# The alpha/beta columns of a projection in four 32-column groups of the array, in fp32

## The chip, the cores and the metric

One core of one Trainium2 chip runs the whole kernel. The metric is device time in microseconds (us), taken as the median of several runs; the profile is one execution taken apart by the hardware profiler.

## The reference, cut to what matters

One layer of a streaming encoder over 1024 positions of width 1024. A conditioning vector gives shift, scale and gate (`mod = silu(c) @ W_ada + b_ada`), the normed input is modulated, and one wide projection feeds both branches:

```python
mod = (cond @ w_ada[l] + b_ada[l])[:, None, :]
sh1, sc1, gt1, sh2, sc2, gt2 = jnp.split(mod, N_MOD, axis=-1)
h = rmsnorm(x, norm1_g[l]) * (1.0 + sc1) + sh1
proj = h @ w_in[l]
qa, ka, va, qkvb, zb, bb, ab, ga, gb = jnp.split(proj, IN_SPLITS, axis=-1)
...
beta = jax.nn.sigmoid(b_raw.astype(jnp.float32))
g = -jnp.exp(a_log.astype(jnp.float32)) * jax.nn.softplus(
    a_raw.astype(jnp.float32) + dt_bias.astype(jnp.float32))
```

`bb` and `ab` (beta and alpha, 4 heads each) are 8 columns of the projection. `qkvb` goes through a causal convolution over four taps and SiLU. Chunked attention, a gated delta rule, the branch merge, an output projection and a SwiGLU feed-forward follow; the change does not touch them.

## The kernel before, in words

**Layout.** Activations lie transposed, features on the 128 partitions, as `act_hi` and `act_lo` of [128, 8, 1024]: the value rounded to fp32r, and what rounding left. The projection goes by units of 128 output columns. A unit's weights (512 KB) land in one of four slots of `w_raw`; ScalarE rounds them to `w_hi` (`split_hi`, line 1666), VectorE forms `w_lo` (`split_lo`, line 2115), both with two slots, and TensorE does three fp32r products (hi by hi, hi by lo, lo by hi) for each of 8 blocks k and each half of 512 positions: 48 matmuls a unit (`dense_k`, line 1164), into `ps[unit % 2]`.

**The start.** Unit 0 holds the 8 alpha/beta columns and 120 others that nobody reads; unit 1 is the first convolved unit. Modulation comes in four parts n; part n gives shift and scale of blocks k = 2n and 2n+1. For a part VectorE sums five of the eight row blocks of `w_ada` (`ada_sum`, lines 2134 and 2136), and TensorE adds the other three and that sum in fp32, four products for each of four column blocks (`modulation`, lines 1217 and 1219). VectorE then scales x (line 2160), ScalarE makes `act_hi` (line 1690), VectorE `act_lo` (line 2165). `units01(n)` multiplies units 0 and 1 with blocks 2n and 2n+1 as they come ready; `beat` fills time on TensorE with small products that nobody reads.

**Units from 2 on** need their split weights (`wlo_ready`) and the bank of the unit two before (`est_ready`). Evacuation of a convolved unit d is a chain: ScalarE copies the bank to `est[d % 2]` (line 1741), then splits the weights of unit d+2; VectorE forms their low part and only then adds three taps (line 2216); ScalarE takes tanh (line 1745); VectorE finishes (line 2221) and raises `est_ready`; GpSimd stores the result (line 1017). From unit 3 on the copy waits for the store of unit d-2:

```python
                    else:
                        act.wait_ge(est_stored[ds % 2], 16 * ((ds - 1) // 2))
```

Ahead of unit 6 TensorE also waits for gate products of GpSimd (line 1263), which follow the store of unit 4.

**DMA order.** Loads are issued by SyncE (SP) in the order of its program, each after its own wait; a waiting instruction holds up all behind it. After the parts of `w_ada` come the weights of units 2 to 5, then a store of x transposed (`xT_d`, 4096 KB, line 615), a store of the attention's bias table (`ext_d`, 1536 KB, line 617, read from 8 partitions, each 128 times over), and the weights of unit 6 (which wait for `wlo_ready` 3) and of the units behind.

```python
                if d == 5:

                    sp.wait_ge(xt_read, NT)
                    sp.dma_start(xT_d.rearrange("(k p) t -> p k t", p=P), xT0[:, :, :]).then_inc(xT_stored, 16)
                    sp.wait_ge(ext_ready, 1)
                    sp.dma_start(ext_d.rearrange("h (p n) -> h p n", n=EXT),
                                 ext[:, :].unsqueeze(1).broadcast_to([A_H, P, EXT])).then_inc(ext_stored, 16)
```

Of the kernel before, what the change touches and what calls it, by code (L numbers as in the profile page):

```python
# [110 lines left out]
def hybrid_layer(nc, x, c, w_ada, b_ada, norm1_g, norm2_g, w_in, rel_rev, w_conv, a_log, dt_bias,  # L111
                 gdn_norm_g, w_branch_a, w_branch_b, w_out, w_ffn_in, w_ffn_out, final_g, out):
    with ExitStack() as ctx:
# [42 lines left out]
        incl = sb("incl", [P, P])  # L156
        after = sb("after", [P, P])
        lvl = sb("lvl", [P, 2, P])
        vT = sb("vT", [P, V_ROWS])
# [375 lines left out]

        ACT_X = (3, 6)

        def ada_count(n):
# [6 lines left out]
        def _(sp):  # L545
# [29 lines left out]
            for t in range(NT):  # L575
                load_x(t)
            load_ada(1)
            for d in range(2):
                load_unit(d, 0, w_in_v, C_AB if d == 0 else C_QKVB + group(1) * P)
            sp.dma_start(rrow[:, :], rel_rev).then_inc(rel_in, 16)  # L580
# [28 lines left out]

            for d in range(2, D_A):  # L610
                load_unit(d, 0, w_in_v, C_QKVB + group(d) * P)
                if d == 5:
# [358 lines left out]
        def _(pool):  # L971
            for s in (yb_free, ya_free):
# [15 lines left out]
                               base=-1, pattern=[[-1, P]], channel_multiplier=1).then_inc(consts_ready, 1)  # L988

            for n, b in enumerate((BLK, 2 * BLK)):  # L990
                odd = lvl[:, n, :].rearrange("p (n two b) -> p n two b", two=2, b=b)[:, :, 1, :]
                nb = P // (2 * b)
                ch.link(pool.memset(odd, 1.0))

                ch.link(pool.affine_select(out=odd, in_=odd, compare_op=ALU.is_ge, fill=0.0, base=0,
                                           pattern=[[-2 * b, nb], [0, b]], channel_multiplier=1))
                ch.link(pool.affine_select(out=odd, in_=odd, compare_op=ALU.is_ge, fill=0.0, base=b - 1,
                                           pattern=[[2 * b, nb], [0, b]], channel_multiplier=-1))
# [157 lines left out]
        def _(pe):  # L1156
# [23 lines left out]
            def in_step(k0, k1):  # L1180
# [3 lines left out]
                return steps + [(d, k) for d in range(2) for k in range(max(k0, 6), k1)]  # L1184

            def units01(n):
                for d, k in in_step(2 * n, 2 * n + 2):
                    if d == 0:
                        pe.wait_ge(lo_ready, k + 1)
                    ins = dense_k(d, k, ps[d], act_hi[:, k, :], act_lo[:, k, :], k == 0, k == 7)  # L1190
                    if k == 7:
                        ins.then_inc(dense_mm, 1)

# [14 lines left out]
            def modulation(n):  # L1208

                pe.wait_ge(ada_in[n], ada_count(n))  # L1210
                pe.wait_ge(asum_ready, n + 1)
                if n:
                    pe.wait_ge(mod_ready, n)
                for q in range(4):
                    dst = gps[:, q * P:(q + 1) * P]
                    for k in range(5, KT):
                        pe.matmul(dst, ada_row(n, k)[:, q * P:(q + 1) * P], cs[:, k:k + 1].broadcast_to([P, P]),
                                  start=(k == 5), stop=False)
                    ins = pe.matmul(dst, asum[:, n % 2, q * P:(q + 1) * P], ones[:, :], start=False, stop=True)
                ins.then_inc(mod_mm, 1)  # L1220
# [14 lines left out]
            modulation(1)  # L1235
            beat(8)
            pe.wait_ge(xt_read, NT)
# [7 lines left out]
            for d in range(2, D_CONV):  # L1245
                for k in range(KT):
                    unit_k(d, 0, k, ps[d % 2])
                if d == 2:

                    pe.wait_ge(ab_read, 1)  # L1250
                    pe.wait_ge(mod_ready, 1)
                    for t in range(NT):
                        ins = pe.transpose(gps[:, t * 8:(t + 1) * 8], est[0:8, 0, t * P:(t + 1) * P],
                                           ident[0:8, 0:8])
                    ins.then_inc(abT_mm, 1)
# [402 lines left out]
        def _(act):  # L1658
# [15 lines left out]
            for t in range(NT):  # L1674
# [5 lines left out]
                if t in ACT_X:  # L1680
                    act.wait_ge(xt_mm, t + 1)
                    act.wait_ge(xt_read, t)
                    act.activation(xT0[:, :, t * P:(t + 1) * P], ps[t % 2][:, :].rearrange("p (k q) -> p k q", k=KT),
                                   ACT.Copy).then_inc(xt_read, 1)
            act.wait_ge(misc_in, 32)
            act.activation(negA[:, :], negA[:, :], ACT.Exp).then_inc(act_chain, 1)
            for n in range(4):
                for k in (2 * n, 2 * n + 1):
                    act.wait_ge(xn_ready, k + 1)
                    act.activation(act_hi[:, k, :], est[:, k % 2, :], ACT.Identity,  # L1690
                                   bias=modT[:, SH1 + k:SH1 + k + 1]).then_inc(hi_ready, 1)
                    if n == 0:
                        split_hi(k)

# [52 lines left out]
            for d in range(D_CONV):  # L1747
                if d == 0:
                    split_hi(2)
                    act.wait_ge(lo_ready, KT)  # L1750
                    act.activation(est[0:8, 0, :], ps[0][0:8, :], ACT.Copy).then_inc(ab_read, 1)
                    continue
# [355 lines left out]
        def _(dve):  # L2108
# [21 lines left out]
            def ada_sum(n):  # L2130
# [3 lines left out]
                ch.link(dve.tensor_scalar(dst, ada_row(n, 0), cs[:, 0:1], None, ALU.mult))  # L2134
                for k in range(1, 5):
                    ins = dve.scalar_tensor_tensor(dst, ada_row(n, k), cs[:, k:k + 1], dst, ALU.mult, ALU.add)
                    if k < 4:
                        ch.link(ins)
# [14 lines left out]
            dve.wait_ge(xt_read, NT)  # L2153
            ada_sum(1)

# [16 lines left out]
            for n in range(4):  # L2172
# [11 lines left out]
                for k in (2 * n, 2 * n + 1):  # L2184
                    norm_scale(k, xT0[:, k, :], gs[:, k:k + 1], aS[:, :], 0)
                if n == 0:
                    split_lo(0)
                    split_lo(1)
                for k in (2 * n, 2 * n + 1):
# [605 lines left out]
```

## Time and profile before

| | |
|---|---|
| median of 3 runs | 1663.96 us (1660.57 to 1665.55) |
| profiled execution, its own time | 1665.2 us |
| its span | 1662.4 us |
| TensorE (PE) busy | 1613.8 us, 97% |
| weight loads (PEld) busy | 1330.6 us, 80% |
| VectorE (DVE) busy | 923.6 us, 56% |
| ScalarE (ACT) busy | 638.8 us, 38% |
| GpSimd (POOL) busy | 268.2 us, 16% |
| chain that ended last, PE's share | 79% |

Times in the trace are microseconds from the start of the span. Matmuls are pipelined, so a group's busy time counts the overlap of neighbours once, and the distance from one start to the next is what a matmul costs. An fp32 product shows as two matmul instructions, an fp32r product as one.

### The profile page before, as it was taken

How to read it: one execution, taken by the hardware profiler on the slowest of the kernel's cores; microseconds unless marked ns; L12 is line 12 of the kernel's file. 1: busy time of each engine (PE TensorE's matmuls, PEld its weight loads, DVE VectorE, ACT ScalarE, POOL GpSimd, SP SyncE). 2: the span in 40 equal slices, each digit the busy share in tenths (PEclk: the TensorE clock that was granted, in tenths of full speed). 3: DMA queues.
4: the chain of work that ended last, by engine and by line, in shares of the span. 5: the costliest groups of instructions: out<-in, count | busy, mean ns of one | idle time of the engine just before them, and what ended most of it. 6: DMA issues, size and time to landing. Idle time of an engine off the chain costs nothing.

```text
span 1662.4 us, 24103 instructions
## 1 busy us (share of the span) xinstructions
PE 1613.8 (97%) x8235; PEld 1330.6 (80%) x8235; DVE 923.6 (56%) x1455; ACT 638.8 (38%) x1308; POOL 268.2 (16%) x284
## 2 busy tenths in 40 slices
PE   5999999999999999999999998999999999999997
PEld 5877878888878787877788887888888888888886
DVE  5777655345444444444653388866666666434424
ACT  4234455555544344444211234333333333322413
POOL 1026571011110101000000012422233220000000
PEclk9999999999999999999999999999999999999999
DMA  9745666555723333422646321222222223653412
GB/s 301 214 114 189 210 188 208 172 181 155 244 87 123 96 107 103 126 95 76 216 134 214 101 64 60 93 88 89 88 76 76 77 87 127 228 174 124 151 45 102
DMA packets 223875, 224.46 MB, mean 135 GB/s; under 512 B 18057, under 2 KB 189194, under 8 KB 223818
## 3 DMA queue, kind: packets, MB, share of 16 engines
q1 hardware_dynamic: 216762, 198.29, 38.1%
q0 software_dynamic: 7056, 25.43, 4.0%
q8 instruction: 33, 0.54, 0.1%
q14 instruction: 24, 0.20, 0.0%
HBM read 163.13 MB, written 60.56 MB: 135 GB/s over the span
## 4 chain that ended last, share of the span: by engine, by line
PE 79%; DVE 3%; DMA 3%; ACT 1%; issue 1%; SPq 0%; DVEq 0%; POOLq 0%; ACTq 0%
PE pm L1560 23%; PE pm L1574 14%; PE pd L1424 11%; PE ps L1164 9%; PE pm L1164 8%; PE sc L1377 2%; PE tT L1400 2%; DMA w_raw<-in_w_in_dram 2%; PE tT L1389 2%; PE pm L1514 1%; PE pm L1472 1%; PE gps L1314 1%; DMA yst<-yb_d 1%; PE gps L1330 1%; PE gps L1348 1%
## 5 line engine op out<-in xcount | busy, mean ns | idle before, releaser
L1164 PE MATMUL ps<-act_hi,w_hi 128*128 128x512 f32 x464 | 155.4, 416 | 3.8 <-DVE act_lo L2165 2.6
L2115 DVE TENSOR_TENSOR w_lo<-w_raw,w_hi 128x1024 fp32r<-128x1024 f32 x61 | 75.7, 1241 | 129.0 <-ACT w_hi L1666 119.2
L1164 PE MATMUL ps<-act_lo,w_hi 128*128 128x512 f32 x464 | 144.9, 394 | 0.0
L1164 PE MATMUL ps<-act_hi,w_lo 128*128 128x512 f32 x464 | 144.5, 393 | 0.0
L1574 PE MATMUL pm<-act_hi,w_hi 128*128 128x512 f32 x352 | 137.2, 390 | 0.0
L1574 PE MATMUL pm<-act_hi,w_lo 128*128 128x512 f32 x352 | 137.0, 389 | 0.0
L1574 PE MATMUL pm<-act_lo,w_hi 128*128 128x512 f32 x352 | 136.9, 389 | 0.0
L1560 PE MATMUL pm<-act_hi,w_hi 128*128 128x512 f32 x320 | 125.7, 393 | 4.7 <-DVE act_lo L2555 3.8
L1560 PE MATMUL pm<-act_lo,w_hi 128*128 128x512 f32 x320 | 125.5, 392 | 0.0
L1560 PE MATMUL pm<-act_hi,w_lo 128*128 128x512 f32 x320 | 125.4, 392 | 0.0
L1424 PE MATMUL pd<-act_hi,w_hi 128*128 128x512 f32 x256 | 111.3, 435 | 0.0
L1164 PEld LDWEIGHTS ps<-act_hi,w_lo 128*128 128x128 f32 x464 | 88.0, 190 | 19.3
L1164 PEld LDWEIGHTS ps<-act_lo,w_hi 128*128 128x128 f32 x464 | 87.7, 189 | 19.4
L1424 PE MATMUL pd<-act_hi,w_lo 128*128 128x512 f32 x256 | 101.0, 394 | 0.0
L1424 PE MATMUL pd<-act_lo,w_hi 128*128 128x512 f32 x256 | 100.3, 392 | 0.0
L1164 PEld LDWEIGHTS ps<-act_hi,w_hi 128*128 128x128 f32 x464 | 81.6, 191 | 20.0 <-issue 7.3
L2673 DVE TENSOR_TENSOR w_lo<-w_raw,w_hi 128x512 fp32r<-128x512 f32 x44 | 30.4, 692 | 117.2 <-ACT w_hi L2017 117.1
L1140 POOL TENSOR_TENSOR est<-w_raw 128x512 f32<-128x512 f32 x20 | 26.3, 1316 | 421.7 <-DVE w_lo L2547 230.2
L1560 PE MATMUL pm<-t_hi,w_hi 128*128 128x512 f32 x240 | 93.4, 389 | 0.0
L1560 PE MATMUL pm<-t_lo,w_hi 128*128 128x512 f32 x240 | 93.4, 389 | 0.0
L1560 PE MATMUL pm<-t_hi,w_lo 128*128 128x512 f32 x240 | 93.4, 389 | 0.0
L1666 ACT ACTIVATE w_hi<-w_raw 128x1024 fp32r<-128x1024 f32 x61 | 64.4, 1055 | 62.7 <-PE pm L1164 49.6
(363 smaller groups left out, 3450.7 us busy)
## 6 DMA issues: line engine op xcount, KB each, us to landing
w_raw<-in_w_in_dram SPq DMA_DIRECT2D x45, 512.0 KB, 5.9
w_raw<-in_w_ffn_in_dram SPq DMA_DIRECT2D x44, 512.0 KB, 3.8
h_raw<-h_d SPq DMA_DIRECT2D x36, 512.0 KB, 3.5
a_raw<-in_w_ada_dram SPq DMA_DIRECT2D x32, 512.0 KB, 4.5
w_raw<-in_w_ffn_out_dram SPq DMA_DIRECT2D x44, 256.0 KB, 3.9
h_d<-hid SPq DMA_DIRECT2D x21, 512.0 KB, 2.7
pk_d<-pk SPq DMA_DIRECT2D x8, 768.0 KB, 3.6
qkva_d<-est POOLq DMA_DIRECT2D x12, 512.0 KB, 6.7
```

The costliest lines, as they stand in the source:

```text
L1140: pool.tensor_tensor(s1, upw[:, 0:4], upw[:, 4:8], ALU.add).then_inc(mix_ready, 1)
L1164: ins = pe.matmul(dst[:, cols], wt[:, ds % 2, k, :], at[:, cols], start=(first and n == 0), stop=(last and n == 2))
L1314: ins = pe.matmul(hd(gps, h), gst[:, (0 if q == Q_QS else 4) + h, :], hd(St, h), start=True, stop=True)
L1377: ins = pe.matmul(score_cols(e, c0, c1), ast[rows, 0, j * P:(j + 1) * P], ast[rows, 1, k0 + c0:k0 + c1], start=True, stop=True)
L1389: ins = pe.transpose(tT[:, kt * P:(kt + 1) * P], Pm[:, e, kt * P:(kt + 1) * P], ident[:, :])
L1400: ins = pe.matmul(tT[rows, 0:P], V[:, j - nk_ + 1 + kt, rows], PT[:, e, kt * P:(kt + 1) * P], start=(kt == 0), stop=(kt == nk_ - 1))
L1424: ins = pe.matmul(pd[:, half(h)], wt[:, ds % 2, kk, :], at[:, kk, half(h)], start=(kk == 0 and n == 0), stop=(kk == KT - 1 and n == 2))
L1560: ins = pe.matmul(bank(n, o), wt[:, c, :], at, start=(c == 0 and x == 0), stop=(c == 3 and x == 2))
L1574: ins = pe.matmul(out_bank(b, h), wt[:, b, :], at[:, j % 8, half(h)], start=(t % NF == 0 and x == 0), stop=(t % NF == NF - 1 and x == 2))
L1666: act.activation(w_hi[:, ds % 2], w_raw[:, ds % NR], ACT.Copy).then_inc(whi_ready, 1)
L2115: dve.tensor_tensor(w_lo[:, ds % 2], w_raw[:, ds % NR], w_hi[:, ds % 2].bitcast(F32), ALU.subtract)\
L2673: dve.tensor_tensor(lo, w_raw[:, raw_o(t) % NR, 0:4], hi.bitcast(F32), ALU.subtract)\
```

## The change

- **Unit 0.** Only 32 columns of its weights are loaded (8 of them are used). They are not split: TensorE multiplies `w_raw` in fp32 with `act_hi` and with `act_lo`. The 16 pairs (block k, hi or lo) are dealt over four groups of 32 output partitions of the same bank, so the array holds four narrow products; the two halves of a pair stand one after the other. `ab_part(n)` has eight such products and comes between unit 1's blocks 2n and 2n+1. The bank's four groups are added when they are transposed: eight fp32 products with `sel` (four identities stacked, made by GpSimd) in place of eight transposes of an 8-row tile.
- **Loads.** The weights of units 0 and 1 are issued ahead of part 1 of `w_ada`. The load of unit 4, which takes unit 0's slot of `w_raw`, waits for unit 0's last product (`dense_mm` 1) in place of its split.
- **Splits.** Unit 1's weights are split as soon as x is read; two counters are raised in place of unit 0's.
- **Modulation.** VectorE sums (5, 0, 4, 4) row blocks in place of (5, 5, 5, 5); TensorE takes the rest. Eight `beat` products go.

```diff
@@ -155,6 +155,7 @@
         after = sb("after", [P, P])
+        sel = sb("sel", [P, 2 * B_H])
         lvl = sb("lvl", [P, 2, P])
@@ -534,6 +535,8 @@
         ACT_X = (3, 6)
+        AB_COLS = 32
+        SUM_ROWS = (5, 0, 4, 4)
@@ -574,9 +577,9 @@
                 load_x(t)
+            sp.dma_start(w_raw[:, 0, :, 0:AB_COLS], w_in_v[:, :, C_AB:C_AB + AB_COLS]).then_inc(raw_in[0], 16)
+            load_unit(1, 0, w_in_v, C_QKVB + group(1) * P)
             load_ada(1)
-            for d in range(2):
-                load_unit(d, 0, w_in_v, C_AB if d == 0 else C_QKVB + group(1) * P)
             sp.dma_start(rrow[:, :], rel_rev).then_inc(rel_in, 16)
@@ -608,6 +611,8 @@
             for d in range(2, D_A):
+                if d == NR:
+                    sp.wait_ge(dense_mm, 1)
                 load_unit(d, 0, w_in_v, C_QKVB + group(d) * P)
@@ -987,6 +992,11 @@
+            pool.wait_ge(consts_ready, 3)
+            ch.link(pool.tensor_tensor(sel[:, :], ident[:, 0:8], ident[:, AB_COLS:AB_COLS + 8], ALU.add))
+            ch.link(pool.tensor_tensor(sel[:, :], sel[:, :], ident[:, 2 * AB_COLS:2 * AB_COLS + 8], ALU.add))
+            pool.tensor_tensor(sel[:, :], sel[:, :], ident[:, 3 * AB_COLS:3 * AB_COLS + 8], ALU.add)\
+                .then_inc(consts_ready, 1)
             for n, b in enumerate((BLK, 2 * BLK)):
@@ -1183,13 +1193,28 @@
+            def ab_part(n):
+
+                if n == 0:
+                    pe.wait_ge(raw_in[0], 16)
+                for k in (2 * n, 2 * n + 1):
+                    for x, at in enumerate((act_hi, act_lo)):
+                        for h in range(2):
+                            c = 2 * k + x
+                            rows = slice(c % 4 * AB_COLS, (c % 4 + 1) * AB_COLS)
+                            ins = pe.matmul(ps[0][rows, half(h)], w_raw[:, 0, k, 0:AB_COLS],
+                                            at[:, k, half(h)].bitcast(F32), start=(c < 4), stop=(c >= 2 * KT - 4))
+                if n == 3:
+                    ins.then_inc(dense_mm, 1)
+
             def units01(n):
-                for d, k in in_step(2 * n, 2 * n + 2):
-                    if d == 0:
-                        pe.wait_ge(lo_ready, k + 1)
-                    ins = dense_k(d, k, ps[d], act_hi[:, k, :], act_lo[:, k, :], k == 0, k == 7)
-                    if k == 7:
-                        ins.then_inc(dense_mm, 1)
+                for k in (2 * n, 2 * n + 1):
+                    pe.wait_ge(lo_ready, k + 1)
+                    if k % 2:
+                        ab_part(n)
+                    ins = dense_k(1, k, ps[1], act_hi[:, k, :], act_lo[:, k, :], k == 0, k == 7)
+                if n == 3:
+                    ins.then_inc(dense_mm, 1)
@@ -1207,16 +1232,19 @@
+                first = SUM_ROWS[n]
                 pe.wait_ge(ada_in[n], ada_count(n))
-                pe.wait_ge(asum_ready, n + 1)
+                if first:
+                    pe.wait_ge(asum_ready, n if n else 1)
                 if n:
...
                     dst = gps[:, q * P:(q + 1) * P]
-                    for k in range(5, KT):
-                        pe.matmul(dst, ada_row(n, k)[:, q * P:(q + 1) * P], cs[:, k:k + 1].broadcast_to([P, P]),
-                                  start=(k == 5), stop=False)
-                    ins = pe.matmul(dst, asum[:, n % 2, q * P:(q + 1) * P], ones[:, :], start=False, stop=True)
+                    for k in range(first, KT):
+                        ins = pe.matmul(dst, ada_row(n, k)[:, q * P:(q + 1) * P], cs[:, k:k + 1].broadcast_to([P, P]),
+                                        start=(k == first), stop=(not first and k == KT - 1))
+                    if first:
+                        ins = pe.matmul(dst, asum[:, n % 2, q * P:(q + 1) * P], ones[:, :], start=False, stop=True)
                 ins.then_inc(mod_mm, 1)
@@ -1233,7 +1261,6 @@
             modulation(1)
-            beat(8)
             pe.wait_ge(xt_read, NT)
@@ -1249,9 +1276,10 @@
                     pe.wait_ge(mod_ready, 1)
+                    pe.wait_ge(consts_ready, 4)
                     for t in range(NT):
-                        ins = pe.transpose(gps[:, t * 8:(t + 1) * 8], est[0:8, 0, t * P:(t + 1) * P],
-                                           ident[0:8, 0:8])
+                        ins = pe.matmul(gps[:, t * 8:(t + 1) * 8], est[:, 0, t * P:(t + 1) * P], sel[:, :],
+                                        start=True, stop=True)
                     ins.then_inc(abT_mm, 1)
@@ -1682,6 +1710,8 @@
                                    ACT.Copy).then_inc(xt_read, 1)
+            act.sem_inc(whi_ready, 1)
+            split_hi(1)
             act.wait_ge(misc_in, 32)
@@ -1689,8 +1719,6 @@
                                    bias=modT[:, SH1 + k:SH1 + k + 1]).then_inc(hi_ready, 1)
-                    if n == 0:
-                        split_hi(k)
@@ -1748,7 +1776,7 @@
                     act.wait_ge(lo_ready, KT)
-                    act.activation(est[0:8, 0, :], ps[0][0:8, :], ACT.Copy).then_inc(ab_read, 1)
+                    act.activation(est[:, 0, :], ps[0][:, :], ACT.Copy).then_inc(ab_read, 1)
                     continue
@@ -2132,9 +2160,9 @@
                 ch.link(dve.tensor_scalar(dst, ada_row(n, 0), cs[:, 0:1], None, ALU.mult))
-                for k in range(1, 5):
+                for k in range(1, SUM_ROWS[n]):
                     ins = dve.scalar_tensor_tensor(dst, ada_row(n, k), cs[:, k:k + 1], dst, ALU.mult, ALU.add)
-                    if k < 4:
+                    if k < SUM_ROWS[n] - 1:
                         ch.link(ins)
@@ -2151,7 +2179,9 @@
             dve.wait_ge(xt_read, NT)
-            ada_sum(1)
+            dve.wait_ge(whi_ready, 1)
+            dve.sem_inc(wlo_ready, 1)
+            split_lo(1)
@@ -2183,9 +2213,6 @@
                     norm_scale(k, xT0[:, k, :], gs[:, k:k + 1], aS[:, :], 0)
-                if n == 0:
-                    split_lo(0)
-                    split_lo(1)
                 for k in (2 * n, 2 * n + 1):
```

## Rows read from the trace of the kernel before

**Rows 1.** The timeline of VectorE (start us, us, what), 28 to 44 us.
```profile
30.82 3.12 DVE L2136 SCALAR_TENSOR_TENSOR asum<-adab,cs,asum 128x512 f32<-128x512 f32 x4
...
34.31 2.47 DVE L2160 SCALAR_TENSOR_TENSOR est<-xT,gs,aS 128x1024 f32<-128x1024 f32 x2
...
39.75 1.23 DVE L2115 TENSOR_TENSOR w_lo<-w_raw,w_hi 128x1024 fp32r<-128x1024 f32 x1 [0.76 <-ACT w_hi L1666]
40.89 2.48 DVE L2165 SCALAR_TENSOR_TENSOR act_lo<-est,modT,act_hi 128x1024 fp32r<-128x1024 f32 x2
```

**Rows 2.** The timeline of TensorE, 28 to 44 us.
```profile
28.71 2.84 PE L1225 MATMUL aT<-ident,ones 128*128 128x128 f32 x24
31.39 1.95 PE L1233 MATMUL aS<-tmp,ones 128*128 128x128 f32 x16
...
42.31 0.70 PE L1164 MATMUL ps<-act_hi,w_hi 128*128 128x512 f32 x2 [2.57 <-DVE act_lo L2165]
```

**Rows 3.** Busy time by stretch: engines, granted clock (PEclk), DMA share, GB/s.
```profile
43.10:46.40 3.30, 3.30 (x9) 2.63 (x8) 3.16 (x6) 0.00 (x0) 0.00 (x0) 0.50 1.14 331
```

**Rows 4.** The timeline of TensorE around one narrow product, columns 64 wide.
```profile
776.03 0.39 PE L1424 MATMUL pd<-act_hi,w_lo 128*128 128x512 f32 x1
776.35 1.31 PE L1400 MATMUL tT<-PT,V 128*64 128x128 f32 x20
777.59 0.50 PE L1424 MATMUL pd<-act_hi,w_hi 128*128 128x512 f32 x1
777.93 0.40 PE L1424 MATMUL pd<-act_lo,w_hi 128*128 128x512 f32 x1
```

**Rows 5.** The timeline of SyncE's queue: start, time to issue, DMA.
```profile
47.92 1.74 SPq L615 DMA_DIRECT2D xT_d<-xT  x1
49.70 1.72 SPq L617 DMA_DIRECT2D ext_d<-ext  x1
72.87 20.69 SPq L550 DMA_DIRECT2D w_raw<-in_w_in_dram  x3
```

**Rows 6.** Busy time by stretch; the last two figures are DMA share and GB/s.
```profile
53.00:61.00 8.00, 8.00 (x50) 7.05 (x49) 7.79 (x10) 2.30 (x2) 0.00 (x0) 1.00 1.02 421
...
64.00:72.00 8.00, 8.00 (x37) 6.64 (x36) 4.02 (x4) 3.78 (x4) 0.00 (x0) 1.00 0.45 48
...
...
93.00:94.00 1.00, 1.00 (x6) 0.83 (x5) 1.00 (x1) 0.00 (x0) 0.00 (x0) 1.00 0.55 164
```

**Rows 7.** Issue to landing of all SyncE loads of line 550 (median and longest of 61).
```profile
DMA to landing us min/median/max: 3.7/5.9/23.7
```

**Rows 8.** Issue to landing of all GpSimd stores of line 1017.
```profile
DMA to landing us min/median/max: 2.9/3.2/13.7
```

**Rows 9.** DMA queues in 84.5 to 85.5 us: packets, MB, share of 16 engines.
```profile
q0 software_dynamic: 50, 0.20, 49.7%
q1 hardware_dynamic: 32, 0.05, 46.0%
```

**Rows 10.** The timeline of ScalarE, 92 to 116 us.
```profile
96.78 1.12 ACT L1741 ACTIVATE est<-ps,wcT 128x1024 f32<-128x1024 f32 x1 [3.85 <-DMA qkvb_d<-est]
...
114.89 1.06 ACT L1745 ACTIVATE tmp<-est 128x1024 f32<-128x1024 f32 x1 [6.14 <-DVE est L2216]
```

**Rows 11.** The timeline of VectorE, 109 to 117 us.
```profile
110.95 3.91 DVE L2216 SCALAR_TENSOR_TENSOR est<-ps,wcT,est 128x1023 f32<-128x1023 f32 x3
115.98 1.23 DVE L2221 SCALAR_TENSOR_TENSOR est<-tmp,est 128x1024 f32<-128x1024 f32 x1 [1.12 <-ACT tmp L1745]
```

**Rows 12.** The timeline of TensorE in three places, 72 to 120 us.
```profile
83.99 0.66 PE L1253 MATMUL gps<-ident,est 8*128 8x8 f32 x8
...
106.03 0.61 PE L1164 MATMUL ps<-act_hi,w_lo 128*128 128x512 f32 x2
106.49 0.65 PE L1164 MATMUL ps<-act_hi,w_hi 128*128 128x512 f32 x2
...
119.25 1.10 PE L1263 MATMUL gps<-gm,after 128*128 128x512 f32 x2 [0.96 <-POOL gm L1027]
```

## The prediction

> **What bounds the kernel now.** The profile table gives TensorE 97% busy and 79% of the chain that ended last, so time is gained only where TensorE works less or stops waiting. I read the timelines of the first 45 us first. VectorE sums rows of `w_ada` for 3.12 us, scales x, waits for ScalarE's split and forms the low weights at 39.75 before it makes `act_lo` at 40.89 [rows 1]; TensorE stands for 2.57 us until 42.31 [rows 2], and then runs at half the granted clock (0.50 in 43.1 to 46.4, the 1.2 GHz level) [rows 3]. Next the DMA order. Behind the weights of unit 5, SyncE issues `xT_d` and the bias table `ext_d` at 47.92 and 49.70; unit 6's weights follow at 72.87 [rows 5]. x transposed moves at 421 GB/s, 4.19 MB in 10.0 us, but the table moves at 48 GB/s with 0.45 of the engines busy, from about 62 until 93 [rows 6], 31 us. So unit 6's load took 23.7 us, to 96.6 [rows 7], and the first GpSimd store, which took 13.7 us to land where 3.2 is the median [rows 8], held ScalarE 3.85 us, until 96.78 [rows 10]. The reader should see that the table's DMA already touches the path, and that unit 6's weights had some 11 us in hand: they landed at 96.6 and were wanted when unit 4's bank had been copied, a pass of 1.1 after TensorE began unit 5 at 106.49 [rows 12].
>
> **TensorE's own work.** Of fp32 at full clock 24 instructions of 128 columns span 28.71 to 31.39, 0.112 us each [rows 2]; fp32r of 512 columns comes every 0.23 (106.03 to 106.49 for two) [rows 12]: 10.9 for the 48 of a unit, which unit 0 loses. No row has 32-column fp32 groups. The nearest is the 64-column product [rows 4]: twenty instructions of 128 columns in 1.31 us, where 0.112 each in turn would be 2.24. So two groups run abreast, although an fp32 product is two instructions on one group: the other group's must have passed a waiting one. Entering and leaving this mode costs (777.93 - 776.03) - 2 x 0.23 - 10 x 0.112 = 0.33. One `ab_part` is 8 products, 16 instructions of 512 columns, 4 x 0.112 = 0.45 each. With four groups abreast it takes 4 x 0.45 + 0.33 = 2.1 us; if a group begins only when the one before has issued its last, 13 x 0.45 + 0.33 = 6.2. Four parts are 8.5 or 24.7 against 10.9. I take 2.1, since the row shows a waiting instruction passed, and keep 6.2 for the range; whether four are passed as well is not shown.
>
> Part 1 on TensorE is 64 fp32 instructions, 7.2 us, where 32 took 3.6; parts 2 and 3 have 40 for 32, 0.9 more each. The eight beats (16 instructions, 1.8) go. The turn to 8 columns is 16 instructions for 8: 1.8 for 0.66 [rows 12]. VectorE loses five operations in part 1 (3.6), one in parts 2 and 3 (0.8 each) and a low split (1.23), ScalarE a split; GpSimd's three adds of 128 x 8 lie in its idle start. ScalarE's copy of 128 rows for 8 has the same 1024 elements a row: nothing.
>
> **The start, added up.** `aS` is done at 31.39 + 1.95 = 33.3. TensorE then takes part 1 (I put the landing of its `w_ada` at about 33 too: 128 KB of unit 0 and the 512 KB of unit 1 go ahead of it) until 40.5. VectorE, with its low split done before 32, scales from 33.4; with 1.24, 1.06 and 1.24 the first low block is ready at about 37, so it is hidden behind part 1: no gap, no half clock. Then 8 steps of unit 1 at 1.36 less the last, 9.5; parts 2 and 3, 9.0; four parts of unit 0, 8.5: unit 0's last product is at T = 40.5 + 27 = 67.5. Unit 2 waits for the split that follows (1.06 + 1.23) and begins at 69.9. Three units and the turn later, 3 x 10.9 + 1.8, unit 5 could begin at 104.4, 2.1 ahead of now.
>
> **What the new wait does.** SyncE's load of unit 4 now waits for T, where before it was out by 46. Behind it stand unit 5's load, `xT_d`, the table, and units 6 and on. Units 4 and 5 have time (their splits are due after about 81 and 94). The table does not: from T, 4 us for the two loads and their start, 10.0 for x, 31 for the table, 1.3 for a store let in between: 113.8. Unit 6's weights land 3.6 after the table's end (96.6 against 93): 117.4, 20.8 later than before. Their chain is ScalarE's split 1.06, low split 1.23, taps 3.91, tanh 1.06, last 1.23 and handoffs 0.1 [rows 10, 11], since the low split stands ahead of unit 4's taps: `est_ready` at 126.0. The gate product came 2.0 after it (119.25 against 115.98 + 1.23): 128.0 for 119.25, **+8.8 us**. TensorE idles before it, first for unit 5, and may fall to half clock: the row of the start priced 3.4 us of it at 1.7. Most would be absorbed by the later wait; I add 0.7 between 0 and 1.7. All later work is behind this point and moves with it. Against the profiled run's own 1665.2: 1674.7. The median was 1.2 lower, so about 1674.
>
> **When the first store lands** decides whether that is all. It would be issued at about 80, while x is moving and the table stands queued. In 84.5 to 85.5 the GpSimd queue moved 50 packets and SyncE's its usual 32 [rows 9]: only the eight engines free of the table served it, the others' half came after 93. So a store does not simply take turns with what is already queued ahead. If what was committed ahead of it then (8.6 us of table and one load) is the engine's depth, it gets in amid the table and lands near 103; unit 3's bank is copied then, unit 5 starts 9.7 later (106.49 - 96.78), 112.8, and unit 6 still binds. If it waits for the whole table it lands at 116.5 or so: a rival.
> The Trainium skill (DMA: Bandwidth & Descriptors, Queues, rings and completion order) says an engine takes turns between queues, packet by packet. By that the store would land at about 85 to 100, and the sum would stay as it is, set by unit 6's weights in SyncE's own queue; the trace agrees only in part, as half the store waited out the table.
>
> **Rivals.**
> - *The store waits out the table.* Landing 116.5, unit 3's bank copied from 116.6, unit 5 at 126.3 for 106.49, +19.8, and 1.7 of half clock: 1686.7. For it: half of the store did so with 8.6 us of table ahead. Against: 29 us of it was never ahead of one.
> - *Groups in turn.* Each part costs 6.2: T and all behind it 16.4 later, 1691; with partial overlap (7 or 10 steps of 0.45) 1680 or 1685. For it: only one waiting instruction is seen passed. Against: two groups are fully abreast.
> The Trainium skill (TensorE: Matmul & The Clock Gate, Part 3: Packing small matmuls) holds that matmuls start and end strictly in program order; that is this rival. The 1.31 us above speak against it.
> - *Faster: the table is quick.* If it needs under about 19 us behind an emptied queue, unit 6's weights land by 106, nothing waits, and the 2.1 ahead at unit 5 stay: 1663. The 31 us decide. For it: its rate was seen in one place only. Against: that rate held for 30 us, beside other loads and alone.
> - *The change doesn't shorten the start* (late `w_ada`, part 1 at half clock): T and the result up to 3 later, 1678.
>
> **Chances.** Forecast 0.42; groups wholly or partly in turn 0.2; store waits out the table 0.18; start not shortened 0.08; table quick 0.12, of which a third only reaches a draw; a hundredth more for a draw by other sums. The range leaves out the fast cases and the two slow rivals together: 1669 to 1692. About 0.3% (5 us) is what a measurement of this kernel can tell from no change: faster 0.08, same 0.05, slower 0.87.
>
> **What would show it.** `ab_part`: 16 narrow instructions in about 2 us (6 if in turn). No gap at TensorE before `units01(0)`, PEclk 1.00 there. `xT_d` and `ext_d` issued after 67, a stretch of 48 GB/s from about 82 to 113, unit 6's load landing near 117, and TensorE idle before unit 5 and before the gate product at 128. The prediction is wrong if the table's stretch is short, if unit 4's load goes out before unit 0 ends, or if later idle time swallows the delay.

## The result, and the profile after

The changed kernel takes **1687.3 us** (median of 4 runs, 1686.0 to 1688.5) for 1663.8 before: ratio 1.0142, 95% interval 1.0127 to 1.0156. It is slower by 23.5 us; the forecast was 1674.0, +10, inside a range up to 1692. The direction held, the size did not. The profiled execution took 1686.0.

The page of the changed kernel, its span and the busy time of each engine:

```profile
span 1684.4 us, 24212 instructions
PE 1632.3 (97%) x8291; PEld 1330.8 (79%) x8291; DVE 916.7 (54%) x1447; ACT 638.8 (38%) x1307; POOL 268.4 (16%) x287
```

TensorE is still 97% busy, but 18.5 us longer than before (1613.8), although the change has shortened its work ahead of unit 2. A wait that moved would have shown as idle time, and PE's idle time grew by only 3.5 us (52.1 for 48.6). So there are two losses, and the second is one of speed.

**First loss: the start.** The timeline of TensorE (start us, us), one `ab_part`, then unit 5 and the gate product:

```profile
42.42 0.62 PE L1205 MATMUL ps<-act_hi,w_raw 128*32 128x512 f32 x1
42.44 0.62 PE L1205 MATMUL ps<-act_lo,w_raw 128*32 128x512 f32 x1
42.45 0.62 PE L1205 MATMUL ps<-act_hi,w_raw 128*32 128x512 f32 x1
42.46 0.62 PE L1205 MATMUL ps<-act_lo,w_raw 128*32 128x512 f32 x1
42.88 0.59 PE L1205 MATMUL ps<-act_hi,w_raw 128*32 128x512 f32 x1
...
44.30 0.73 PE L1174 MATMUL ps<-act_hi,w_hi 128*128 128x512 f32 x2
...
109.43 1.04 PE L1174 MATMUL ps<-act_hi,w_hi 128*128 128x512 f32 x2 [4.30 <-DVE est L2248]
...
129.86 2.04 PE L1291 MATMUL gps<-gm,after 128*128 128x512 f32 x2 [6.99 <-POOL gm L1037]
```

Four groups start within 0.04 us of each other and the 16 instructions take 1.9 us: four abreast. The gate product comes at 129.86 for 119.25 [rows 12], 10.6 later. The queue of SyncE, and then ScalarE, show why:

```profile
67.91 0.99 SPq L553 DMA_DIRECT2D w_raw<-in_w_in_dram  x2
68.95 0.89 SPq L620 DMA_DIRECT2D xT_d<-xT  x1
69.89 2.15 SPq L622 DMA_DIRECT2D ext_d<-ext  x1
72.08 45.40 SPq L553 DMA_DIRECT2D w_raw<-in_w_in_dram  x3
```

```profile
99.79 1.12 ACT L1769 ACTIVATE est<-ps,wcT 128x1024 f32<-128x1024 f32 x1 [8.30 <-DMA qkvb_d<-est]
...
113.85 1.12 ACT L1769 ACTIVATE est<-ps,wcT 128x1024 f32<-128x1024 f32 x1 [5.67 <-DMA qkvb_d<-est]
119.33 1.06 ACT L1694 ACTIVATE w_hi<-w_raw 128x1024 fp32r<-128x1024 f32 x1 [4.36 <-DMA w_raw<-in_w_in_dram]
```

The table left SyncE at 69.9, not 49.7 [rows 5]. The first store of GpSimd was issued at 79.65 and held ScalarE until 99.79; unit 6's weights held it until 119.33. The waits for a store are that of [rows 10] grown; the one for the weights is new. TensorE ran at half clock behind both of its gaps (PEclk 0.52 in 109.5 to 112.9, 0.50 in 130.0 to 133.3).

**Second loss: the pace.** Busy time by stretch, before: 825 to 865 lies in the merge, 895 to 955 in the output projection, 1060 to 1400 in the feed-forward part. TensorE never pauses in them; the number in brackets behind its busy time counts its instructions:

```profile
825.00:865.00 40.00, 40.00 (x178) 33.14 (x177) 23.19 (x20) 7.42 (x7) 0.00 (x0) 1.00 0.46 155
895.00:955.00 60.00, 60.00 (x266) 49.67 (x265) 23.44 (x21) 13.88 (x14) 0.00 (x0) 1.00 0.37 115
1060.00:1400.00 340.00, 340.00 (x1502) 281.53 (x1501) 229.48 (x324) 115.74 (x197) 88.70 (x65) 1.00 0.26 86
```

The same stretches after:

```profile
825.00:865.00 40.00, 40.00 (x173) 32.14 (x172) 23.29 (x20) 7.43 (x7) 0.00 (x0) 1.00 0.50 166
895.00:955.00 60.00, 60.00 (x266) 49.70 (x265) 17.24 (x16) 11.88 (x12) 0.00 (x0) 1.00 0.51 173
1060.00:1400.00 340.00, 340.00 (x1473) 276.23 (x1472) 227.00 (x320) 112.93 (x193) 93.31 (x68) 1.00 0.25 81
```

At a granted clock of 1.00 in all six, the merge does 173 products where it did 178, the feed-forward part 1473 for 1502, and the output projection the same 266. From one start to the next a 512-column product takes 226.7 ns before, everywhere from 825 on; after, 233.3 in the merge, 226.7 in the output projection and 231.1 in the feed-forward part. Measured at equal instructions of ScalarE, the kernel is 9 us behind from 330 to 780, 11 behind at 900, 12 at 1050 and 22 at the end.

No line of that code was changed. What changed is where its tiles lie: the new tile `sel`, 32 bytes in each partition, stands ahead of `lvl` and moves every tile declared behind it by 32 bytes: `y_hi` (the merge's input), `t_hi` and `w3_hi` (moving operand and weights of the feed-forward part) and the rest. `act_hi`, `act_lo`, `w_raw`, `w_hi` and `w_lo` stay.

### The profile page after: what moved, and what is told of

It reads as the page before. It is cut to its first block, busy times and chain, and to the rows that moved or that the text cites. A ratio compares the mean times of both kernels' runs of the same rounds, so it can differ in the third digit from the quotient of the medians.

```text
span 1684.4 us, 24212 instructions
## 1 busy us (share of the span) xinstructions
PE 1632.3 (97%) x8291; PEld 1330.8 (79%) x8291; DVE 916.7 (54%) x1447; ACT 638.8 (38%) x1307; POOL 268.4 (16%) x287
## 4 chain that ended last, share of the span: by engine, by line
PE 82%; DVE 3%; DMA 1%; ACT 1%; issue 1%; SPq 0%; DVEq 0%; ACTq 0%
PE pm L1588 23%; PE pm L1602 14%; PE pd L1452 11%; PE ps L1174 10%; PE pm L1174 9%; PE sc L1405 2%; PE tT L1428 2%; PE pm L1542 2%; PE tT L1417 2%; PE pm L1500 1%; DMA w_raw<-in_w_in_dram 1%; PE gps L1342 1%; PE gps L1358 1%; PE gps L1376 0%; PE gps L1362 0%
## 5 line engine op out<-in xcount | busy, mean ns | idle before, releaser
L1174 PE MATMUL ps<-act_lo,w_hi 128*128 128x512 f32 x448 | 140.4, 395 | 0.0
L1174 PE MATMUL ps<-act_hi,w_lo 128*128 128x512 f32 x448 | 139.9, 394 | 0.0
```

The lines of the kernel that those rows point to most:

```text
L1174: ins = pe.matmul(dst[:, cols], wt[:, ds % 2, k, :], at[:, cols], start=(first and n == 0), stop=(last and n == 2))
```

## The experiments

Fifteen kernels; the ratio is to the kernel before, with its 95% interval.

### Placement alone, wait alone

```diff
         after = sb("after", [P, P])
+        sb("unused", [P, 8])
```

> The kernel before with one unused tile of 32 bytes per partition where the changed kernel has its new tile, and nothing else. Theory A (of the 22 us, some 12 come from the address: the merge's and the feed-forward's operands stand 32 bytes off a multiple of 64, and a 512-column matmul comes every 233 ns in place of 227): slower by 11 to 13 us, 1676; nothing before 780 us of the span moves, and the start keeps its times. Theory B (the late slowdown comes with the changed order of work): 1664, and a spacing of 227 throughout.

Measured: 1677.0, ratio 1.0081 (1.0059 to 1.0103). 32 bytes that nobody touches cost 13 us. 825 to 865 and 1060 to 1400:

```profile
825.00:865.00 40.00, 40.00 (x173) 32.12 (x172) 21.98 (x19) 7.43 (x7) 0.00 (x0) 1.00 0.47 155
...
1060.00:1400.00 340.00, 340.00 (x1473) 276.03 (x1472) 224.34 (x316) 112.33 (x192) 89.55 (x66) 1.00 0.25 80
```

173 and 1473, the counts of the changed kernel.

The other half, the kernel before with only the wait:

```diff
             for d in range(2, D_A):
+                if d == NR:
+                    sp.wait_ge(dense_mm, 1)
                 load_unit(d, 0, w_in_v, C_QKVB + group(d) * P)
```

> The kernel before with only the new wait: the load of unit 4 waits for unit 0's last product, which is at 70.4 us here against 67.8 in the changed kernel. Theory A (the wait alone makes the stall): table and unit 6's load 2.7 us later than in the changed kernel, gate product of unit 6 near 132.5, time 1664 + 12 = 1676. Rival (the wait costs only together with the rest of the change): 1664.

Measured: 1680.3, ratio 1.0105 (1.0088 to 1.0122), 4 us more than expected and far from the rival's 1664. Products take 226.7 ns from 825 on, and the profiled execution is 16.3 us behind at 155 to 290 and 14.8 at the end. The wait alone costs more than in the change; there T, the end of unit 0, comes 3.6 us later (unit 4's load goes out at 71.56 for 67.91). TensorE stood 8.35 us before unit 5 and 4.84 before the gate product. ScalarE's first copy behind the store:

```profile
106.48 1.12 ACT L1743 ACTIVATE est<-ps,wcT 128x1024 f32<-128x1024 f32 x1 [12.44 <-DMA qkvb_d<-est]
```

### What about the placement?

The changed kernel with 32 unused bytes behind `sel`, so that all lies at multiples of 64 bytes again:

> The changed kernel with 32 unused bytes behind the new tile, so that all that follows stands on a multiple of 64 again. Theory A: 1687 falls to 1675, the gate product of unit 6 stays at 129.9 us of the span, and the difference to before stays at 9 to 11 us from there to the end. Theory B: 1687.

Measured: 1684.4, ratio 1.013 (1.0113 to 1.0147): a miss. The pace of the feed-forward part became 229.7, not 226.7. Multiples of 64 bytes are not it. So two runs with nothing moved or with 64 bytes moved. `sel` put into a tile that is free then:

```diff
-        sel = sb("sel", [P, 2 * B_H])
+        sel = beta[:, 0:2, :].rearrange("p t h -> p (t h)")
```

> The changed kernel with the eight summing columns kept in a part of the tile beta that nothing else uses by then, so that every tile lies where it lay before. Theory A (the slow spacing of the 512-column fp32r products comes from where the tiles lie): spacing 226.7 ns everywhere as before, only the loss of the start is left, 9 to 10 us: about 1674. Rival (the slow spacing comes from the change itself, by its timing or its code, since the run with 64 bytes of displacement still had 229.7 ns): 229.7 ns again and 1682 to 1684.

Measured: 1674.0, ratio 1.007 (1.0045 to 1.0094); 1501 instructions in 1060 to 1400. This is the change without any displaced tile, as the forecast had it, and at its time.

> The kernel before with an unused tile of 64 bytes in each partition ahead of the tile of levels, so that all later tiles move by 64 bytes and nothing else changes. If what counts is where a tile lies within 128 bytes (or more): spacing 229 to 230 ns in the merge and after 1000 us, as in the run of the changed kernel with 64 bytes, some 3 ns of 227 on about 570 us of products: +7, about 1671. If only the place within 64 bytes counts: 226.7 ns and 1664.

Measured: 1674.9, ratio 1.0065 (1.0048 to 1.0082), 228.9 ns in the merge and 229.8 in the feed-forward part. My reading was then that the place within 128 bytes counts:

> The kernel before with an unused tile of 128 bytes in each partition ahead of the tile of levels. Theory (what counts is where the operands lie within 128 bytes): spacing 226.7 ns everywhere as before, 1663 to 1665. Rival (what counts is the distance to the tiles that don't move, or any displacement at all): 229 to 233 ns in the merge and from 1000 us on, 1671 or more.

Measured: 1674.4, ratio 1.0053 (1.0036 to 1.007), 232.4 ns in the merge and 230.7 in the feed-forward part. The theory fell, and its rival, the distance to the tiles that don't move, was left. Two runs that tell distance from place: 128 unused bytes ahead of everything, and 128 bytes behind `act_hi` and `act_lo`.

```diff
+        sb("unused", [P, 32])
         act_hi = sb("act_hi", [P, KT, S], F32R)
```

> The kernel before with an unused tile of 128 bytes in each partition ahead of the first tile, so that all tiles move by 128 bytes together. Theory (what counts is the distance between the tile of the weights and the tile of the moving operand, which stays the same here): 226.7 ns everywhere, 1663 to 1665. Rival (what counts is where a tile lies in itself): 229 to 233 ns again somewhere, 1671 or more.

Measured: 1663.8, ratio 0.9994 (0.9979 to 1.0009): no change, with every tile 128 bytes further.

```diff
         act_lo = sb("act_lo", [P, KT, S], F32R)
+        sb("unused", [P, 32])
         w_raw = sb("w_raw", [P, NR, KT, P])
```

> The kernel before with the 128 unused bytes behind the tiles act_hi and act_lo, ahead of the raw and split weights and all the rest, so that only act_hi and act_lo stay. Theory (distance between weights and moving operand): the mirror image of the run with 128 bytes ahead of the tile of levels. There the merge was slow (y moved, w_hi not: 232.5 ns) and the output projection fast (act and w_hi, neither moved). Here the merge is fast, 226.7 to 227.5 ns (y and w_hi both moved), and the output projection (890 to 960 us) and the first units (60 to 220 us) are slow, 229 ns or more: 1669 to 1680. Rival (place in itself, or a property of the tiles y and t): the merge stays slow, the first units and the output projection stay at 226.7 ns.

Measured: 1681.0, ratio 1.0097 (1.0073 to 1.0121), the top of the range expected. The products of the units in 60 to 120 take 232.4 ns, where the kernel before has 227.4. The three stretches again, of this kernel:

```profile
825.00:865.00 40.00, 40.00 (x178) 33.13 (x177) 23.79 (x20) 7.62 (x8) 0.00 (x0) 1.00 0.46 149
895.00:955.00 60.00, 60.00 (x259) 48.27 (x258) 20.53 (x18) 12.61 (x12) 0.00 (x0) 1.00 0.39 131
1060.00:1400.00 340.00, 340.00 (x1476) 276.71 (x1475) 224.68 (x319) 113.02 (x193) 91.39 (x67) 1.00 0.24 79
```

The mirror image. With 128 bytes ahead of `lvl` (the run two above) the first two rows read:

```profile
825.00:865.00 40.00, 40.00 (x173) 32.42 (x173) 22.89 (x19) 7.42 (x7) 0.00 (x0) 1.00 0.39 127
895.00:955.00 60.00, 60.00 (x267) 49.69 (x266) 21.66 (x19) 12.61 (x12) 0.00 (x0) 1.00 0.42 136
```

There y had moved and the weights had not: the merge is slow (173), the output projection fast (267). Here y and the weights moved together and `act_hi` stayed: the merge is fast (178), the output projection slow (259, 233.3 ns). What counts is the distance between the moving operand and the weights of TensorE.

**A control inside one kernel.** The feed-forward loop alternates two moving tiles (`act` and `t`) and two tiles of weights (`w_hi` and `w3_hi`; the trace leaves the 3 out). In the changed kernel `t` and `w3_hi` moved, `act` and `w_hi` did not. Its timeline of TensorE, one line at each turn; 24, 24, 24 and 12 products lie between them:

```profile
1061.11 0.39 PE L1588 MATMUL pm<-act_hi,w_hi 128*128 128x512 f32 x1
...
1066.57 0.40 PE L1588 MATMUL pm<-t_hi,w_hi 128*128 128x512 f32 x1
...
1072.17 0.40 PE L1588 MATMUL pm<-act_hi,w_hi 128*128 128x512 f32 x1
...
1077.77 0.39 PE L1588 MATMUL pm<-t_hi,w_hi 128*128 128x512 f32 x1
...
1080.52 0.39 PE L1588 MATMUL pm<-act_hi,w_hi 128*128 128x512 f32 x1
```

By the order of the program (`op_slot`) these stretches are act with `w_hi` (5.46 us for 24, 227.5 ns each), t with `w_hi` (233.3), act with `w3_hi` (233.3) and t with `w3_hi` (229.2). Over 1060 to 1400, away from the turns, the means are 227.3, 233.4, 233.1 and 228.3 ns. In the kernel with the weights displaced by 128 bytes they are 233.6, 226.9, 233.5 and 227.3: only act had stayed there. So the same tile is fast with one partner and slow with the other, in one kernel and within microseconds, which a property of a tile or of the code can't do. The two pairs that kept their distance are still 0.2 to 1.6 ns above 226.7, which no run explains.

### The start: order, own tile, table

Stores ahead of unit 4's waiting load (`if d == 3` for `if d == 5`, on the kernel with the 64 bytes):

> The aligned changed kernel with the stores of x transposed and of the bias table issued ahead of the load that waits for unit 0. Theory A (all of the remaining loss is the late table): the load of unit 6 lands near 97, the copy of unit 3's bank is held by the first store to 96.8 as before, unit 5 starts at 106.5, and the time is 1664, a draw: the start is 2 us sooner and gives it back at unit 5. Rival (the new start costs something of its own, or the table isn't the cause): 1669 or more. Second rival (the store isn't held): 1661.

Measured: 1677.6, ratio 1.0081 (1.0064 to 1.0098): 6.9 us less than the same kernel without it, where 20 less had been expected. The miss has two parts. One is the pace, which takes some 9 us behind 770. The other is that unit 4's load, issued at 68.3, now stood behind the table itself:

```profile
94.16 1.06 ACT L1695 ACTIVATE w_hi<-w_raw 128x1024 fp32r<-128x1024 f32 x1 [9.43 <-DMA w_raw<-in_w_in_dram]
```

TensorE stood 8.18 us before unit 4 (until 102.79). So: no wait for a product at all, the raw columns in a tile of their own (`sel` in `beta` in all that follow):

```diff
+            ab_w = sbin(st0, "ab_w", [P, KT, 32])
...
-            sp.dma_start(w_raw[:, 0, :, 0:AB_COLS], w_in_v[:, :, C_AB:C_AB + AB_COLS]).then_inc(raw_in[0], 16)
+            sp.dma_start(ab_w[:, :, :], w_in_v[:, :, C_AB:C_AB + AB_COLS]).then_inc(raw_in[0], 16)
...
                 if d == NR:
-                    sp.wait_ge(dense_mm, 1)
+                    sp.wait_ge(raw_in[0], 16)
```

> As the run with the summing columns in beta, and the raw columns of the alpha/beta unit in a tile of their own, at the end of the start's tiles, so that unit 4's load no longer waits until the last of the column-group products has read them (it waits only until they have landed). Theory (the loss of the start is this one wait, through the order of the load, the copy of x and the table): the loads go out as in the kernel before, unit 2 still starts 1.1 us sooner, no gap of 4 or 7 us: 1662 to 1664. Rival (the column-group products or the moved splits cost something themselves behind the start): 1667 or more.

Measured: 1665.5, ratio 1.0013 (1.0002 to 1.0024), above the 1662 to 1664 expected and below the rival's 1667. The wait was nearly all of the start's loss. The gain of the shorter start is not there either: ScalarE's copy of unit 3 waited for the first store until 97.88 (96.78 before, [rows 10]), so TensorE stood 2.0 us before unit 5 and was then 1.1 us behind the kernel before.

The spread table, on that kernel; the source is a small copy, so that the outermost dimension has 128 entries and not 8:

```diff
-                    sp.dma_start(ext_d.rearrange("h (p n) -> h p n", n=EXT),
-                                 ext[:, :].unsqueeze(1).broadcast_to([A_H, P, EXT])).then_inc(ext_stored, 16)
+                    sp.dma_start(ext_s, ext[:, :]).then_inc(ext_stored, 16)
...
+                    sp.wait_ge(ext_stored, 16)
+                    sp.dma_start(ext_d.rearrange("h (p n) -> p h n", n=EXT),
+                                 ext_s.unsqueeze(0).broadcast_to([P, A_H, EXT])).then_inc(ext_stored, 16)
```

> As the run with the raw columns in a tile of their own, with the table first copied small (12 KB) and then spread from there over the partitions as the outermost dimension, so that 16 DMA engines write it and not 8. Theory (PE is busy without a break from 42 to 118 us, the table only holds ACT's copies): the table is done sooner, but the time stays within 1 us of the run without this: 1662 to 1664. Rival (the table's stretch still holds unit 2's or 3's store and through it PE): 2 to 4 us less than that run.

Measured: 1661.1, ratio 0.9982 (0.9973 to 0.9992), 4.4 less than without: the rival. The same table on the kernel before:

> The kernel before with the spread table alone (a small copy first, then written by 16 DMA engines), nothing of the change. Theory (in the kernel before PE runs without a break from 42 to 118 us, so the slow table costs it nothing there; it is only behind the shorter start of the change that the table comes onto the path): 1662 to 1664, no change. Rival (the gain of 4.4 us of the spread table lies in the table itself, whatever the start): 1659 to 1660.

Measured: 1660.6, ratio 0.9978 (0.9961 to 0.9995): the rival again. The slow table costs the kernel before some 3 us. Its profile no longer has the gap of 0.96 ahead of the gate product [rows 12], which comes at 117.38, 1.9 sooner (in the run above at 115.89, 3.4 sooner); the rest lies in waits of 1 to 2 us between 250 and 370 that come and go from kernel to kernel, and was not pinned down.

The table spread, with the wait of the change kept, decides what the wait costs by itself:

> The changed kernel with the summing columns in beta (1674.0 us) and the table spread by 16 DMA engines, with the wait for the column-group products kept. Theory (the wait costs only because the loads behind it land behind the slow table): the gap of 3 to 4 us ahead of unit 5 shrinks to 1 us or less and the one of 7 to 10 us ahead of the gate product too, 1662 to 1665. Rival (the delay of the loads by the wait itself is what costs, whatever the table takes): 1670 or more.

Measured: 1658.8, ratio 0.9966 (0.9953 to 0.998), 15.2 us under the same kernel with the slow table and lower than the theory's 1662 to 1665. The version with the own tile and no such wait took 1661.1, so behind a quick table the wait costs nothing that these runs can tell. Both gaps are gone, though its table too was issued late, at 73.9. Busy time by stretch, of this kernel; the last two figures are DMA share and GB/s:

```profile
84.00:90.00 6.00, 6.00 (x28) 4.95 (x27) 4.30 (x4) 1.60 (x2) 0.00 (x0) 1.00 1.06 387
90.00:96.00 6.00, 6.00 (x29) 4.95 (x28) 2.65 (x6) 2.48 (x3) 0.54 (x1) 1.00 1.04 306
96.00:102.00 6.00, 6.00 (x28) 4.99 (x27) 4.98 (x4) 0.88 (x2) 0.00 (x0) 1.00 0.01 4
```

By 96 the table and the loads around it are through, on full engines, where the old table alone took 31 us at 48 GB/s and 0.45 of the engines [rows 6]. The Trainium skill (DMA: Bandwidth & Descriptors, Why a DMA increments its semaphore by 16 and not by 1) gives the rule: the number of DMA engines is the largest one up to 16 that divides the outermost dimension (longer than 1) of both sides. By it 8 heads outside use 8 engines and 128 partitions 16; the shares 0.45 and 1.06 agree. Two things were changed together, the outermost dimension and the source (a copy in DRAM in place of 8 SBUF partitions); no run parts them, and only the share of the engines points to the first.

### The packing, and the sums

Two column groups for four (`c % 2`), on the version with own tile and spread table:

> As the fastest version so far (summing columns in beta, raw columns in their own tile, spread table), with the alpha/beta products dealt over two column groups of the array and not four. Theory (the groups run abreast, so a part of 16 products costs 4 passes of 0.43 us with four groups and 8 with two): a part takes 3.6 to 3.9 us for 2.1, unit 2 starts 6 to 7 us later and all behind it: 1667 to 1668. Rival (the products follow one another whatever the group, or the start is held by another engine): 1661 to 1662.

Measured: 1666.0, ratio 1.0011 (0.9996 to 1.0026), 5.0 more, a little less than expected. A part runs from 44.21 to 47.79, 3.6 us for 1.9, which is 6.8 for the four.

Five rows of parts 2 and 3 summed on VectorE, as before (`SUM_ROWS = (5, 0, 5, 5)`), on the same version:

> As the fastest version so far, with five and not four of the raw rows of parts 2 and 3 of the modulation summed on DVE, as in the kernel before (part 1 stays on TensorE). PE loses 16 narrow products, 2 times 0.9 us by the rows of the timeline; DVE gains 2 times 0.75 us ahead of the scaling of two columns. Theory (PE sets the start from the first product on): unit 2 starts 1 us sooner, 1660. Rival (DVE's sums stand ahead of the columns that PE waits for): 0 to 1.5 us later, 1661 to 1662.5.

Measured: **1657.5**, ratio 0.9956 (0.9941 to 0.9971), the fastest of all and 6 us under the kernel before. Unit 2 starts at 68.27 for 69.47, the 1.2 us foreseen; the median fell by 3.6, and the profiled runs (1659.0 and 1658.1) don't show more, so the size beyond 1.2 is left open. Half of the 6 us is the table's: against the kernel before with the quick table (1660.6) this version is 3.1 us faster, and the one with four rows summed (1661.1) not at all.

## Why the prediction was right or wrong

**Packing: right.** 2.1 us a part were forecast, 1.9 measured; the four groups start within 0.04 us, though in the program twelve instructions of other groups stand ahead of the last one's first. The rival of groups in turn (6.2) is out. The Trainium skill (TensorE: Matmul & The Clock Gate, Part 3: Packing small matmuls), by which matmuls start strictly in program order, does not hold for this row.

**The start: right.** T = 67.5 forecast, 67.9 measured; unit 2 at 69.9 forecast, 70.4 measured; no half clock ahead of unit 1's products.

**What the wait does: right in cause, 2 us short.** Unit 6's weights were wanted from ScalarE at 119.33, forecast 117.4; the gate product came +10.6 for +8.8. Of the 1.9 us, 0.4 is T and the rest the transfers; from the weights on the chain took the time forecast (10.5 for 10.6). The term of 0.7 for the clock was low too: half clock followed both gaps, and behind the gate product the kernel is 12.3 behind. The first store landed at about 99.7, amid the table, where I had put 103, so that the rival in which it waits out the table (1686.7) is out, although the total came near its time: a right number for a wrong reason. The run without displacement measures this part alone: 1674.0, the forecast. That hit has luck in it, since its profile has the gate product at 132.6, 13.4 late, and wins 5 us of that back in later waits, which I had not counted on.

**What failed: the placement.** The step is the one that costed what the change adds, where the new tile `sel` got no term for its 32 bytes (only GpSimd's three adds were priced, at nothing); "All later work is behind this point and moves with it" took the pace of that work as given. The 32 bytes measured +13.1 us alone in the kernel before (1677.0 for 1663.8) and 13.3 in the changed one (1687.3 for 1674.0), so they account for all that the result has beyond the start's 10.2. The 512-column products of the merge and the feed-forward part take 233.3 and 231.1 ns in place of 226.7.

**"The table is quick: 1663."** A rival I gave 0.12, as a condition the kernel doesn't fulfil. Made true by hand, it gave 1658.8. The mechanism of the start is thereby shown from both sides: the wait costs 8.5 us (1674.0 against 1665.5, where it is lifted) to 16 us (alone, in the kernel before) with the slow table, and nothing with a quick one.

## What to carry to other kernels

A tile added in the middle of the declarations moves all that follow, and may slow code that the diff doesn't touch: compare the spacing of equal matmuls far from the change before looking for waits, and put small new tiles last or into dead ones. When a wait is put ahead of a queue of transfers, look for the slowest transfer behind it: making that one quick (here its outermost dimension from 8 to 128) gave 3 us by itself and 15 behind the wait. A rate of half the engines in a row of DMA shares is a defect to mend, not only a number for the forecast.

## What the runs showed of the hardware

- The pace of fp32r matmuls of 512 columns depends on the distance in SBUF between the moving operand and the weights.
